# One list of prompt and sample attention blocks, with the bias added in PSUM by VectorE

## The reference

```python
def diff_attention(q, k, v, qpos, kpos, lam, rel_bias):
    s = jnp.einsum('bqhmd,bkhmd->bhmqk', q, k, ...) * (DA_DK ** -0.5)
    bias = rel_bias[rel_bucket(kpos[None, :] - qpos[:, None])]
    visible = (kpos[None, :] // CHUNK) <= (qpos[:, None] // CHUNK)
    p = jax.nn.softmax(jnp.where(visible, s + bias, -jnp.inf), axis=-1)
    attn = p[:, :, 0] - lam * p[:, :, 1]
    return jnp.einsum('bhqk,bkhd->bqhd', attn.astype(v.dtype), v)
```

## Time and profile before

| what | us |
|---|---|
| median of 3 runs | 1752.15 |
| lowest and highest run | 1750.01, 1755.09 |
| time of the profiled execution | 1755.83 |
| its span in the trace | 1754.0 |
| prompt attention in the trace | 540.6 to 675 |
| sample attention in the trace | 675 to 752 |
| TensorE busy, share of the span | 93% |

### The profile page before, as it was taken

One profiled execution on the slowest core, in us unless ns is written; L12 is line 12 of the kernel. 1 busy time (PEld: TensorE's weight loads), 2 busy tenths in 40 slices (PEclk: granted clock), 3 DMA queues, 4 the chain that ended last, 5 costly groups with the idle time before them and its releaser, 6 DMA issues.

```text
span 1754.0 us, 23438 instructions
## 1 busy us (share of the span) xinstructions
PE 1634.1 (93%) x9297; PEld 1445.9 (82%) x9297; DVE 991.9 (57%) x1568; ACT 640.6 (37%) x1155; POOL 447.1 (25%) x263
## 2 busy tenths in 40 slices
PE   4899998699998897798999999999999999999996
PEld 3688896589996665676799999999988989889875
DVE  3775318642014665435676666666556677667844
ACT  4422123211113553354432222223444444444532
POOL 0121124231210001035753333333441121112232
PEclk8899999789999998989999999999999999999998
DMA  9554110221213003724642222222264335444452
GB/s 326 195 174 161 37 27 1 54 76 47 64 52 126 1 1 96 245 94 135 192 152 67 66 61 61 70 63 85 84 173 140 121 115 157 142 152 122 143 168 70
DMA packets 163858, 189.10 MB, mean 108 GB/s; under 512 B 7850, under 2 KB 126867, under 8 KB 163730
## 3 DMA queue, kind: packets, MB, share of 16 engines
q1 hardware_dynamic: 139626, 132.11, 24.5%
q10 hardware_dynamic: 18748, 37.79, 6.9%
q0 software_dynamic: 5376, 17.71, 2.9%
HBM read 170.48 MB, written 17.11 MB: 107 GB/s over the span
## 4 chain that ended last, share of the span: by engine, by line
PE 50%; DVE 5%; DMA 3%; ACT 1%; POOL 1%; issue 1%; ACTq 0%; DVEq 0%
PE PS L641 10%; PE PS L643 10%; PE PS L642 10%; PE PS L1105 4%; PE PS L1107 4%; PE PS L1106 4%; PE PS L564 1%; PE PS L1034 1%; PE PS L1035 1%; PE PS L1036 1%; DMA k_cache<-in_cache_k_dram 1%; DMA x_new<-in_x_prompt_dram 1%; DVE y_new L1617 1%; DMA weights_raw<-in_w_up_dram 1%; DVE y_tmp L1623 1%
## 5 line engine op out<-in xcount | busy, mean ns | idle before, releaser
L2308 POOL TENSOR_TENSOR weights_lo<-weights_raw,weights_hi 128x1024 fp32r<-128x1024 f32 x103 | 267.9, 2602 | 740.9 <-ACT weights_hi L1827 740.8
L641 PE MATMUL PS<-h_hi,weights_hi 128*128 128x384 f32 x1280 | 435.5, 340 | 3.6 <-DVE h_lo L1196 3.2
L642 PE MATMUL PS<-h_lo,weights_hi 128*128 128x384 f32 x1280 | 432.7, 338 | 0.0
L643 PE MATMUL PS<-h_hi,weights_lo 128*128 128x384 f32 x1280 | 432.6, 338 | 0.0
L1827 ACT ACTIVATE weights_hi<-weights_raw 128x1024 fp32r<-128x1024 f32 x202 | 213.4, 1058 | 160.4 <-PE PS L1107 99.1
L641 PEld LDWEIGHTS PS<-h_hi,weights_hi 128*128 128x128 f32 x1280 | 242.9, 190 | 12.6 <-issue 12.4
L642 PEld LDWEIGHTS PS<-h_lo,weights_hi 128*128 128x128 f32 x1280 | 242.9, 190 | 0.1
L643 PEld LDWEIGHTS PS<-h_hi,weights_lo 128*128 128x128 f32 x1280 | 242.6, 190 | 0.0
L1105 PE MATMUL PS<-weights_hi,g_hi 128*128 128x512 f32 x396 | 160.2, 405 | 8.8 <-POOL g_lo L2439 5.3
L1107 PE MATMUL PS<-weights_hi,g_lo 128*128 128x512 f32 x396 | 157.9, 399 | 0.0
L1106 PE MATMUL PS<-weights_lo,g_hi 128*128 128x512 f32 x396 | 157.0, 397 | 0.0
(11 more groups left out here) (396 smaller groups left out, 2528.3 us busy)
## 6 DMA issues: line engine op xcount, KB each, us to landing
weights_raw<-in_w_up_dram SPq DMA_DIRECT2D x88, 512.0 KB, 3.9
weights_raw<-in_w_down_dram SPq DMA_DIRECT2D x66, 512.0 KB, 4.2
w_ada_unit<-in_w_ada_dram SPq DMA_DIRECT2D x32, 512.0 KB, 5.5
weights_raw<-in_w_in_dram SPq DMA_DIRECT2D x24, 512.0 KB, 5.3
weights_raw<-in_w_out_dram SPq DMA_DIRECT2D x24, 512.0 KB, 3.9
w_ada<-in_w_ada_dram SPq DMA_DIRECT2D x4, 2048.0 KB, 16.7
k_cache<-in_cache_k_dram ACTq DMA_DIRECT2D x8, 1024.0 KB, 5.4
y_new<-x_scratch ACTq DMA_DIRECT2D x9, 512.0 KB, 6.1
```

The costliest lines, as they stand in the source:

```text
L641: pe.matmul(out, wh, xh, start=(i == 0), stop=False)
L642: pe.matmul(out, wh, xl, start=False, stop=False)
L643: mm = pe.matmul(out, wl, xh, start=False, stop=(i == n - 1))
L2308: mark(gp.tensor_tensor(WL[n % 3][:, :], WR[:, n % 3, :], WH[n % 3][:, :].bitcast(F32), ALU.subtract), "w_lo")
```

## The change

Prompt blocks and samples become one list `WORK` of 40 items: the 32 prompt blocks in the old order, and a sequence ahead of prompt blocks 5, 9, 13, 17, 21, 25, 28 and 31. All engines run one software pipeline over it, with the stages as before. Each of the four key turns of a sequence stands at the head of one of the four items ahead of it; all are copied by ScalarE, into one buffer. Score banks are three pairs taken in turn, a wide block taking two; banks 6 and 7 are taken in turn by all key turns, turns and value products. The bias and the mask are kept as one float32 tile `BIASP`, and VectorE adds it to the last 256 columns in PSUM ahead of each maximum; `IDR`, `BH` and `BL` are gone. The score products are issued with the map outside and the piece of 512 keys inside. The caches are loaded by SP, the values into one buffer; POOL sets up zeroes and query blocks; the five copies into `ATS` are one. One `phase_end` is left. Units 24 to 26 are split (ScalarE high, POOL low) behind the last item. In `YH` the attention half now stands first, so that `OT` can lie over it.

```diff
+        SAMPLE_BEHIND = [5, 9, 13, 17, 21, 25, 28, 31]
+        WORK = []
+        for t, hi in enumerate(PROMPT):
+            WORK += [("s", SAMPLE_BEHIND.index(t))] if t in SAMPLE_BEHIND else []
+            WORK.append(("p", t))
...
+        KEY_STEPS = {w - NH + h: (b, h) for b, w in enumerate(SAMPLE_AT) for h in range(NH)}
...
+            def caches_in():
+                sp.wait_ge(sem("proj"), 72)
+                for b in range(NB):
+                    if b >= 2:
+                        sp.wait_ge(sem("aux"), USE["key", b - 2, 3] + 1)
+                    sp.dma_start(KC[:, b % 2, :, :], a["cache_k"][0, b].rearrange("(k p) h n -> p k (h n)", p=P))\
+                      .then_inc(sem(f"kc_in{b % 2}"), 16)
+                    if b >= 1:
+                        sp.wait_ge(sem("aux"), USE["values", SAMPLE_AT[b - 1], 0] + 1)
+                    sp.dma_start(VC[:, :, :], a["cache_v"][0, b].rearrange("(k p) h n -> p k (h n)", p=P))\
+                      .then_inc(sem("vc_in"), 16)
+
             for n in range(2, NU):
+                if n == N_OUT0 + 3:
+                    caches_in()
...
-                for c0 in range(0, W, 512):
-                    c1 = min(W, c0 + 512)
-                    for m in range(2):
-                        pe.matmul(PS[:, S[m] + c0 // 512, 0:c1 - c0], QT[m * DK:(m + 1) * DK, h, i * P:(i + 1) * P],
-                                  KTT[m * DK:(m + 1) * DK, h, c0:c1], start=True, stop=c1 <= lo)
                 for m in range(2):
-                    cuts = sorted({lo, min(W, (lo // 512 + 1) * 512), W})
-                    for b0, b1 in zip(cuts, cuts[1:]):
-                        out = PS[:, S[m] + b0 // 512, b0 % 512:b0 % 512 + b1 - b0]
-                        pe.matmul(out, IDR[:, :], BH[:, h, 2 * P - W + b0:2 * P - W + b1], start=False, stop=False)
-                        mm = pe.matmul(out, IDR[:, :], BL[:, h, 2 * P - W + b0:2 * P - W + b1], start=False, stop=True)
+                    for c0 in range(0, W, 512):
+                        c1 = min(W, c0 + 512)
+                        mm = pe.matmul(PS[:, S[m] + c0 // 512, 0:c1 - c0], QT[m * DK:(m + 1) * DK, h, i * P:(i + 1) * P],
+                                       KTT[m * DK:(m + 1) * DK, h, c0:c1], start=True, stop=True)
                     mm.then_inc(sem("scores"), 1)
...
+            def aux_free(of):
+
+                if USE[of] >= 2:
+                    pe.wait_ge(*emptied(USES[USE[of] - 2]))
+
+            def key_turn(b, h):
...
+                if h == 0:
+                    pe.wait_ge(sem(f"kc_in{b % 2}"), 16 * (b // 2 + 1))
+                aux_free(("key", b, h))
...
+            for w in range(NW + 3):
+                if w in KEY_STEPS:
+                    key_turn(*KEY_STEPS[w])
+                if w < NW:
+                    if SCORES_FREE[w]:
+                        pe.wait_ge(sem("exp"), SCORES_FREE[w])
+                    (scores if WORK[w][0] == "p" else scores_s)(w)
+                if 2 <= w < NW + 2:
+                    if WORK[w - 2][0] == "p":
+                        attn_turn(w - 2, 0)
+                    else:
+                        attn_turn_s(w - 2)
+                if w >= 3:
+                    (attn_values if WORK[w - 3][0] == "p" else attn_values_s)(w - 3)
+                if 2 <= w < NW + 2 and pieces(w - 2) == 2:
+                    attn_turn(w - 2, 1)
...
+            def row_max(w):
+                t = WORK[w][1]
+                W = tile_width(w)
+                for m in range(2):
+                    ve.wait_ge(sem("scores"), 2 * t + m + 1)
...
+                    near = PSF[:, c0 + max(0, W - 2 * P):c0 + W]
+                    ch(ve.tensor_tensor(near, near, BIASP[:, PROMPT[t][0], 2 * P - min(W, 2 * P):], ALU.add))
+                    mark(ve.tensor_reduce(MX[:, 2 * (t % 2) + m:2 * (t % 2) + m + 1], PSF[:, c0:c0 + W], AX.X,
+                                          ALU.max, negate=True), "row_max")
...
+            for w in range(NW + 3):
+                if w < NW:
+                    (row_max if WORK[w][0] == "p" else row_max_s)(w)
+                if 1 <= w < NW + 1:
+                    (combine if WORK[w - 1][0] == "p" else combine_s)(w - 1)
+                if w >= 3 and WORK[w - 3][0] == "s":
+                    o_rows(w - 3)
...
+            for w in range(NW + 3):
+                if w in KEY_STEPS:
+                    key_out(*KEY_STEPS[w])
+                if 2 <= w < NW + 2:
+                    if WORK[w - 2][0] == "p":
+                        turn_out(w - 2, 0)
+                    else:
+                        turn_out_s(w - 2)
+                if w >= 3 and WORK[w - 3][0] == "p":
+                    o_out(w - 3)
+                if w < NW:
+                    (exps if WORK[w][0] == "p" else exps_s)(w)
+                if 2 <= w < NW + 2 and pieces(w - 2) == 2:
+                    turn_out(w - 2, 1)
+                if w >= NW:
+                    ac.wait_ge(sem("scores"), 2 * len(PROMPT))
+                    w_hi(N_OUT0 + w - NW)
```

More of the change, by code:

```diff
@@ new lines, in build, with tile_width @@
+        NW = len(WORK)
+        SAMPLE_AT = [WORK.index(("s", b)) for b in range(NB)]
+        PROMPT_AT = [WORK.index(("p", t)) for t in range(NH * NPT)]
+        def tile_width(w):
+            kind, t = WORK[w]
+            return (PROMPT[t][1] + 1) * P if kind == "p" else PAST + TS
+        PAIRS, EXPS, SCORES_FREE = [], [], []
+        pair_at, pair_user = 0, [None] * 3
+        for w, (kind, t) in enumerate(WORK):
+            wide = kind == "p" and tile_width(w) > 512
+            mine = [(pair_at + n) % 3 for n in range(1 + wide)]
+            pair_at += len(mine)
+            PAIRS.append(mine)
+            users = [pair_user[p] for p in mine if pair_user[p] is not None]
+            SCORES_FREE.append(max((EXPS[u][-1] for u in users), default=0))
+            done = EXPS[-1][-1] if EXPS else 0
+            EXPS.append([done + n + 1 for n in range(2 if kind == "p" else 1)])
+            for p in mine:
+                pair_user[p] = w
@@ new lines, in score_bank, with pieces @@
+        def score_bank(w, m):
+            return 2 * PAIRS[w][m] if len(PAIRS[w]) == 2 else 2 * PAIRS[w][0] + m
+        KEY_STEPS = {w - NH + h: (b, h) for b, w in enumerate(SAMPLE_AT) for h in range(NH)}
+        assert len(KEY_STEPS) == NB * NH
+        def pieces(w):
+            return 1 + (WORK[w][0] == "p" and tile_width(w) > 512)
+        USES = []
+        for w in range(NW + 4):
+            if w in KEY_STEPS:
+                USES.append(("key",) + KEY_STEPS[w])
+            if 2 <= w < NW + 2:
+                USES.append(("turn", w - 2, 0))
+            if 3 <= w < NW + 3:
+                USES.append(("values", w - 3, 0))
+            if 2 <= w < NW + 2 and pieces(w - 2) == 2:
+                USES.append(("turn", w - 2, 1))
@@ new lines, in build, with emptied_by, emptied @@
+        USES.append(("last_rows", 0, 0))
+        USE = {of: u for u, of in enumerate(USES)}
+        def emptied_by(of):
+            kind, n, m = of
+            if kind == "key":
+                return "keys_out"
+            if kind == "values":
+                return "o_out" if WORK[n][0] == "p" else "o_rows"
+            return "turn_out"
+        EMPTIED = {of: (emptied_by(of), sum(emptied_by(v) == emptied_by(of) for v in USES[:u + 1])) for u, of in enumerate(USES)}
+        def emptied(of):
+            name, n = EMPTIED[of]
+            return sem(name), n
@@ L978, in _ @@
[L978 to L987 removed]
+                W = (i + 1) * P
@@ L990, in _ @@
                 mm.then_inc(sem("scores_s"), 1)
[L991 to L995 removed]
+            def aux_free(of):
+                if USE[of] >= 2:
+                    pe.wait_ge(*emptied(USES[USE[of] - 2]))
+            def key_turn(b, h):
+                if (b, h) == KEY_STEPS[1]:
+                    pe.wait_ge(sem("kv_rows"), 8)
+                if h == 0:
+                    pe.wait_ge(sem(f"kc_in{b % 2}"), 16 * (b // 2 + 1))
+                aux_free(("key", b, h))
+                bank = aux_bank(("key", b, h))
+                for k in range(4):
+                    mm = turn(PS[:, bank, k * P:(k + 1) * P], KC[:, b % 2, k, h * P:(h + 1) * P])
+                mm.then_inc(sem("aux"), 1)
@@ new lines, in attn_values @@
+            def attn_values(w):
+                t = WORK[w][1]
+                h, i = PROMPT[t]
+                pe.wait_ge(*emptied(("turn", w, pieces(w) - 1)))
+                aux_free(("values", w, 0))
+                bank = aux_bank(("values", w, 0))
+                for k in range(i + 1):
+                    mm = pe.matmul(PS[:, bank, 0:P], VTOK[:, k, h * DV:(h + 1) * DV],
+                                   ATB[t % 2][:, k * P:(k + 1) * P], start=(k == 0), stop=(k == i))
+                mm.then_inc(sem("aux"), 1)
@@ new lines, in attn_values_s @@
+            def attn_values_s(w):
+                b = WORK[w][1]
+                pe.wait_ge(*emptied(("turn", w, 0)))
```

(9 more changed lines are left out.)

448 lines of the change are left out of this document (168 added, 280 removed).

## The result

The changed kernel takes 1738.08 us (median of 4 runs, 1737.12 to 1740.02) where the kernel before took 1753.62 (4 runs). The ratio is 0.9915, 95% interval 0.9895 to 0.9935: 15.5 us faster, more than the 0.3% that the prediction counts as a difference. I had said 1716, with 1690 to 1736 as the range. The direction held. The gain is less than half of the one forecast, and the time lies 2 us outside the range. Of all executions reported here one, of e5_key_behind, was slow (2666 us at a clock of 0.555); its ratio leaves it out.

A forecast was written before the change was run, and what follows sets the result against it. Bound: a round of scores, maxima, exponentials, copy and next turn through three engines, none full. 4 x 39.2 + 8.5 + 9.4 = 174.7 from 540.7 ends the stage at 715.4, not 752.0: -36.6, so 1716 us; range 1690 to 1736.

The forecast's parts named there:

- the caches: Key and value loads through SP's queue: 8.5 us exposed, 5.5 for the eighth sequence, 2 for the seventh, 1 for others.
- the walk of the round: Each engine stepped in order through one head of the joined list: 39.2 us a head, 32 work and 7 waiting.
- the tail: From the last scores to the stage's end: 11.2 us, with one POOL low part; 9.4 on top of four heads.
- My rival of 7.2 us for each sequence: Keys land late for every sequence by the full 7.2 us, 58 in place of 8.5; 1765; chance 0.04.
- The additions: VectorE's 64 bias additions ahead of the maxima: 0.43 us for 256 columns, 28.7 us of VectorE in all.
- VectorE's load: VectorE's work for prompt and samples in the joined stage: 131 us in all.
- the 75% that I had named as a sign: Sign that would show the forecast: VectorE over 75% busy in the joined stage.
- TensorE's scores of a head: TensorE's score products in one head: 9.3 us, each width by its share of 1.91.
- The last block: The full last stretch of 989 us, whose work the change does not touch: can only move as a block.
- Query blocks and zeroes: POOL's set-up while the first blocks run: covered by some 20 us ahead of the first sequence's scores.
- Row halves: Rival: new score order stops the two maps' row halves running side by side; 18 us in all, 1728 to 1734; chance 0.10.
- The low clock: Rival: TensorE's clock falls in the joined stage to 0.83, its 127 us grow by 25; 1736; chance 0.06.

The follow-up runs named there:

- e5_key_behind: Changed kernel with the key turn in the item of a sequence's values, and ScalarE's copy of it, behind those values; 1730.79 us, ratio 0.9878 to the kernel before.
- e1: Changed kernel with SP issuing each K load ahead of the V load it stood behind; 1719.73 us, ratio 0.9815 to the kernel before.
- e6: Changed kernel with the edits of e1, e2 and e5_key_behind together; 1725.44 us, ratio 0.9853 to the kernel before.
- e9: Changed kernel with the edits of e1 and e5_key_behind, and the copy o_rows on ScalarE ahead of its exponentials; 1714.94 us, ratio 0.9780 to the kernel before.
- e10: Changed kernel with the edit of e1, and the low parts of units 24 to 26 on VectorE instead of POOL; 1717.39 us, ratio 0.9789.
- e11: Changed kernel with the edits of e9 and e10 together; 1709.76 us, ratio 0.9752 to the kernel before.
- e2: Changed kernel with POOL's meeting at the end of the attention phase ahead of its three low parts; 1734.27 us, ratio 0.9902 to the kernel before.
- e4: Kernel before, its two attention parts kept, with VectorE's bias addition in place of the identity products; 1764.16 us, ratio 1.0101 to the kernel before.
- e7: Changed kernel with the old order of the score products, piece outside and map inside; 1731.45 us, ratio 0.9890 to the kernel before.
- e3: Changed kernel with the identity products for the bias back in the joined list and no addition on VectorE; 1736.31 us, ratio 0.9908 to the kernel before.

## Why the prediction was wrong, point by point

In the trace the stage and its tail end at 735.1 and not at 715.4: 19.7 us missing. Three terms of the sum were too small, all on the same side: the caches, where I took a part of the transfer as caught up; the walk of the round, which lacks a wait; and the tail, where I counted one low part for three. The mechanism, one pipeline whose rounds stay short of full engines, was right.

**The caches (8.5; measured 15.8 of waits, and 16.3 given back by e1 up to the last score).** This is the largest. My term had 5.5 for the eighth sequence, 2 for the seventh and 1 for the rest. TensorE's waits in the trace are 8.3 us for the eighth, 3.8 for the seventh, 1.5 and 0.3 for two middle ones and 1.9 for the first. I saw that K stands behind V in the queue and then took a transfer's time less "what the other engines catch up". Nothing was caught up: the chain that ended last runs through the transfer for 7.82 us, and the clock was low behind it. The transfer itself is long because the values go out 0.4 us ahead of it: a load of keys with nothing ahead of it took 5.1 us in e1 (issued at 555.89), one behind a load of values 7.4 us or more in the changed kernel. The mechanism was right, the size was not. My rival of 7.2 us for each sequence stayed wrong, since two blocks do cover the keys of most.

**The round (39.2 a head; measured 41.2 without key waits).** The step that failed is the walk between tiles 1 and 5. It has a wait of 1.0 at tile 5 for a bank "whose copy is behind tile 6's exponentials". It lacks the like of it one item earlier: the values of a sequence need the bank of the key turn at the head of the same item, which ScalarE copies behind the exponentials of the item before. That costs TensorE 6.4 us in six waits, the longest 1.60, and tile 5 starts at 21.7 in the changed kernel where the walk had 20.6. e5, e6 and e9 show that with this wait alone removed the one for `o_rows` takes its place (a head stays at 42.3), and that with both gone a head is 39.4 to 39.5 and the walk fits within 0.3 at each of the eight starts. Over the stage it is 4 to 6 us: to the last score 162.1 in e1 and 158.3 in e9, and 161.6 in e10 and 156.0 in e11, the pair without a middle head at the lower clock. The other waits of the walk, the one for the combination above all (5.7 us in five), stand in the trace.

**The tail (11.2; measured 15.6 from the end of the last scores, 719.5, to 735.1).** I counted one low part of 2.60 on POOL behind one high part. The three low parts stand in a row there, 6.95 us, since ScalarE begins their high parts at 726.98, 728.41 and 730.00, and POOL is slower than that. What lies ahead of POOL's first low part, 8.7 us (719.5 to 728.18), is what I had for it (7.6 and 1.06), so the whole miss of 4.4 is 6.95 in place of 2.60. With the low parts on VectorE (e10) the last square stands 4.5 us nearer to the last score, and e2 gives nothing: the squares that come earlier are slowed by POOL in their turn. The Trainium skill says of this, in "SBUF — State Buffer", section "SBUF: two separate sides", that VectorE and GpSimd share a pair of ports as an exclusive lock: an instruction of VectorE with two inputs in SBUF, beside one of GpSimd that reads SBUF, needs it, and so does one in a two-port mode, and whichever starts second is blocked until the first has ended. The trace agrees: the product of the row sums takes 1.78 us beside POOL and 0.19 without it, and it ends at 730.59, when POOL's first low part has ended at 730.54; the instruction behind it ends at 732.88, and POOL's second low part at 732.84.

Up to the end of the last scores the walk has 156.8 - 1.8 = 155.0 without the caches and the changed kernel 179.0. Of these 24.0 e1 gives back 16.3, 7.8 more than the term for the caches, though 1.5 of it is in the first head and not the queue's doing (38.8 us at a clock of 0.87 in the changed kernel, 37.3 at 0.95 in e1, and the same 37.3 in e2, which has the changed kernel's queue); e11 another 6.1, the waits of the round and the lower clock in one of e1's middle heads; and 1.6 stay in e11, which still waits 2.4 for the first keys. With the 4.4 of the tail that is 7.8 + 6.1 + 1.6 + 4.4 = 19.9, and the stage began 0.2 us earlier than in the kernel before: 19.7. That only 1.6 stay is partly luck. I took the head with two sequences four times, but the first head has one and the last has three: in e11 the first takes 36.7 and the last, to the end of its scores, 41.0 where the sum has 37.4.

**What held.** The additions: 256 columns took 0.43, as estimated. What they do to a round did not hold in the separate lists: the gain of the narrow blocks is missing (e4). VectorE's load over the first five stretches is 28.25 + 30.51 + 30.55 + 30.69 + 7.74 = 127.7, where I had 131; in a stage of 194.6 us that is 66%, not the 75% that I had named as a sign. TensorE's scores of a head, 9.3 in the sum, are 8.6 by the shares that I gave (36/8 of 1.91); no term of the time rests on it. The last block is rigid (988.80). Query blocks and zeroes on POOL were hidden. Row halves run side by side: 1.99 us for eight passes in the new order, and no gain from the old one (e7). By the Trainium skill, "TensorE: Matmul & The Clock Gate" (Part 3: Packing small matmuls), the halves would have stood in strict order; here the trace and e7 both say otherwise, and the measurement decides. The low clock, a rival of its own, was not what made the difference: the middle heads ran at 1.00, and the last head's 0.88 became 1.00 when its key waits went (e1).

**What the change was worth.** The joined list, with all that was moved along with it, made the gain, and the addition on VectorE made none of it: e3, the joined list with the identity products, has the same time, and in the separate lists the addition costs 8.7 us by the trace and 0.6 to 1.4% by the runs (e4). In the joined list TensorE gets 4.4 us a head back and VectorE gets 6.4 more to do (30.5 against 24.1). That the two cancel because both are in every round fits these rows and is not shown by itself.

**The range.** It took each rival alone. No case had several terms of the sum wrong at once with the same sign, although all three were worked out as "transfer or chain less what is hidden", which can only err to one side when the cover is thinner than thought.

## What to carry to other kernels

When a load goes into a queue behind another, ask when the buffer of the one ahead becomes free, and count the whole transfer as exposed where fewer blocks lie between than it takes; the remedy is the order in the queue. When a wait for a bank is removed, look for the next owner of that bank: here removing one wait gave nothing, and removing both gave 1.8 us a head. Work of POOL at a seam is not hidden by moving it past the seam if VectorE has work there: count what the two take side by side.

## What the runs showed of the hardware that I had not expected

- POOL and VectorE beside each other hold each other up: a product of 32 columns 0.19 to 1.78 us, a pair of squares of 384 columns 1.1 to 3.18, three low parts on POOL 6.95 to 9.15. In the changed kernel each of VectorE's two held-up instructions ended 0.04 to 0.05 us behind a low part of POOL's. A copy out of PSUM on VectorE at 728.59 in the changed kernel, beside the same work of POOL, kept its 0.29.
- A wait of 8.33 us on TensorE costs more than itself: the next score products of a sequence took 1.96 us, at a clock of 0.50, where they take 1.08.
- A low part of 1024 columns takes VectorE 1.22 us and POOL 2.32 to 2.60.
- A load of 1 MB of keys landed in 5.1 us alone and in 7.4 to 8.1 when a load of values of the same size had gone out 0.4 us ahead of it in the same queue (5.2 to 5.7 for that one); at 600.51, where both took longer, 7.1 and 9.2.
